# The second layer's modulation columns move from up projections to down projections

## The chip, the core and the metric

One core of a Trainium2 chip runs the whole program. The metric is device time in microseconds, from 1894.69 to 1894.86 in three runs of the kernel before, 1894.77 in the median.

Engines are called TensorE (PE in the profile, PEld its weight loads), VectorE (DVE), ScalarE (ACT), GpSimd (POOL) and SyncE (SP).

## What is computed

Two blocks of a sequence model in float32, on 512 tokens of width 1024: the first with stick-breaking and gated linear attention and a convolutional feed-forward network, the second with two layers (pooling and grid attention in one, an mLSTM in the other), each with its own feed-forward network. The layers of the second block are modulated by a condition `c`:

```python
    cond = jax.nn.silu(c)
    for layer in range(DEPTH_2):
        mod = cond @ ada_w[layer] + ada_b[layer]
        sh1, sc1, g1, sh2, sc2, g2 = jnp.split(mod, 6, axis=-1)
        h = modulate(rms_norm_2(x), sh1, sc1)
        ...
        x = x + g1[:, None, :] * y
        h = modulate(rms_norm_2(x), sh2, sc2)
        x = x + g2[:, None, :] * swiglu(h, ffn_w1[layer], ffn_w3[layer], ffn_w2[layer])
```

`ada_w` is 2 x 1024 x 6144 numbers, 50 MB. The product has one row, and the kernel does not give it to TensorE.

## The kernel before, in words

**Stages and chunks.** The program is a list of stages, each of some chunks of weights. The three feed-forward networks (FFN) are called by a prefix: none for the first block's, `e_` and `o_` for the two layers of the second. Each has two halves of an up and a down stage: `up0`, `down0`, `up1`, `down1`, and so on. An up stage has 11 chunks of 48 matmuls of 512 columns, a down stage 8 chunks of 33. Activations lie as 128 x 512 tiles, 8 of them for a width of 1024.

**One chunk.** SyncE loads weights into one of two `raw` slots. ScalarE rounds them into `wh` (`hi_part`, L514), always 2048 columns. GpSimd takes the difference `raw - wh` into `wl` (L2386), 1408 columns in a down stage and 2048 in an up stage; for `pool_u`, the stage behind `down1`, and a few others it does so in four instructions of 512 (L2396). TensorE multiplies three times (`wh` and `wl` by the high part of the input, `wh` by the low part). It starts a chunk when `lo_done` says that GpSimd is through, and when the chunk two before has been drained from PSUM. `hi_part` of the next chunk waits for the end of the chunk before the present one, whose slot it takes.

**Draining a down chunk.** VectorE adds the result to the residual tile `h` (L691, L692). Where a norm follows the stage (`down1`, `e_down1`), `hi_only` has ScalarE square and scale the tile of the chunk before (`tile_act`, L231 to L240), and VectorE adds the square to a running sum and forms the low part (`tile_dve`, L258, L263, L266). `down1` needs two sums, of x and of the scaled x, so three operations on each engine; `e_down1` needs two. At the start of the next stage TensorE takes the sum over partitions (`norm_sum_pe`, L379).

**Modulation.** The 96 columns of `mod` (48 for each layer, 128 numbers each) are sums on VectorE: `ada_dve` (L856) multiplies a 128 x 1024 tile of `ada_w`, loaded into one of four slots, by the condition and accumulates along the row. They are spread over stages by the table `ADA_OF`: one a chunk in `out` and `att_out` (4 each), two a chunk in `up0`, `up1`, `e_up0` and `e_up1` (22 each). `ada_load` (L849) issues the 512 KB load for a column from ScalarE's queue in the up stages, from SyncE's in `out` and `att_out`; it waits until the sum that last used the slot is done. Each engine takes its instructions in the order in which the program lists them, so a load that waits holds what stands behind it on ScalarE. `mod_dve` adds the bias for a layer, of layer 0 ahead of `down1`, of layer 1 ahead of `e_down1`.

Of the kernel before, what the change touches and what calls it, by code (L numbers as in the profile page):

```python
# [92 lines left out]
def build(nc, xT, w2048, w1024, w1408, ada, c_d, par_d, cst_d, gla_d, rope_d, pool_d, outT):  # L93
    with ExitStack() as ctx:
# [99 lines left out]
        GQ_SQ = [arena[:, 8, :], arena[:, 9, :]]  # L194
        GQ_ACC = arena[:, 15, :]
        RSTD = arena[:, 30, :]
# [451 lines left out]
        def hi_only(a, stage):  # L648
# [4 lines left out]
            def body(c, slot, l):  # L653
                if not (KIND[stage] == "D" and is_static(l) and l == 0):
                    hi_part(a, c + 1, 1 - slot)
                if norm and KIND[stage] == "D":
                    if is_static(l) and l == 0:
                        return
                    a.wait_ge(drained, c)
                    tile_act(a, norm, l - 1, 1 - slot)  # L660
                elif norm:
                    a.wait_ge(res_half, l + (HALF_OF[stage] + 1))
                    tile_act(a, norm, l * 2, 0)
                    a.wait_ge(drained, c + 1)
                    tile_act(a, norm, l * 2 + 1, 1)
            if norm:
                chunk_loop(a, stage, body, hi=3)
                chunk_loop(a, stage, body, lo=3, hi=COUNT[stage] - last)
# [16 lines left out]
        def drain_residual(v, stage, gate=None):  # L685
# [29 lines left out]
            if norm:  # L715
# [5 lines left out]
                chunk_loop(v, stage, body, lo=1, hi=2)  # L721
                chunk_loop(v, stage, body, lo=2)
                tile_dve(v, norm, KT - 1, (C0[stage] + KT - 1) % 2 if KIND[stage] == "D" else 1)
# [23 lines left out]
        def ada_first(a, stage):  # L747
            for l in range(2):
                ada_load(a, stage, (C0[stage] + l) % 2, l)

        def up_act(a, stage):
# [6 lines left out]
            def body(c, slot, l, ahead=True, open_=True):  # L758
# [17 lines left out]
                a.activation(zh[:, bass.ds(l, 1), :], HID[:, slot:slot + 1, :], ACT.Copy).then_inc(hid_hi, 1)  # L776
                if stage in ADA_OF and not (is_static(l) and l + 2 >= HALF):
                    ada_load(a, stage, slot, l + 2)
# [10 lines left out]
        def up_dve(v, stage):  # L789
# [4 lines left out]
            def body(c, slot, l):  # L794
# [17 lines left out]
                else:  # L812
# [4 lines left out]
                                zh[:, bass.ds(l, 1), :].bitcast(F), ALU.subtract).then_inc(drained, 1)  # L817
                if stage in ADA_OF:
                    ada_dve(v, stage, slot, l)
            if stage in NORM_INTO and not first:  # L820
                chunk_loop(v, stage, body, hi=1)
                chunk_loop(v, stage, body, lo=1)
            else:
# [8 lines left out]

        ADA_OF = {"out": (0, 1), "up0": (4, 2), "up1": (4 + 2 * HALF, 2), "att_out": (ADA_M, 1),
                  "e_up0": (ADA_M + 4, 2), "e_up1": (ADA_M + 4 + 2 * HALF, 2)}

        def ada_at(stage, slot, l, i):

            first, each = ADA_OF[stage]
            A = l * each + (first + i)
            if is_static(A):  # L840
                return A, A % ADA_SLOTS
            return A, (first + i + each * ((slot + C0[stage]) % 2)) % ADA_SLOTS

        def ada_load(sp, stage, slot, l):
            for i in range(ADA_OF[stage][1]):
                A, at = ada_at(stage, slot, l, i)
                if not (is_static(A) and A < ADA_SLOTS):
                    sp.wait_ge(ada_done, A - (ADA_SLOTS - 1))
                sp.dma_start(ada_raw[:, at, :], ada[bass.ds(A, 1), :, :].rearrange("a p n -> p (a n)")  # L849
                             ).then_inc(ada_full[at], 16)  # L850

        def ada_dve(v, stage, slot, l):
            for i in range(ADA_OF[stage][1]):
                A, at = ada_at(stage, slot, l, i)
                v.wait_ge(ada_full[at], A * 4 + (16 - 4 * at))
                v.scalar_tensor_tensor(ada_raw[:, at, :], ada_raw[:, at, :], 1.0, cond_row[:, :], ALU.mult, ALU.mult,  # L856
# [1561 lines left out]
        def _(a):  # L2418
# [13 lines left out]
            a.wait_ge(drained, end_of("up1"))  # L2432
            a.dma_start(ROPE[:, :, :], rope_d.rearrange("p (a t) -> p a t", t=T)).then_inc(rope_in, 16)
# [31 lines left out]
        def _(v):  # L2465
# [29 lines left out]
            for i in range(2):  # L2495
# [194 lines left out]
```

## Time and profile before

| | |
|---|---|
| median of three runs | 1894.77 us |
| profiled execution, span from first to last instruction | 1893.4 us (its full time isn't shown apart) |
| TensorE busy | 1874.5 us, 99% |
| VectorE, ScalarE, GpSimd busy | 905.8, 751.5, 775.2 us |
| granted TensorE clock | 1.000 |
| modulation sums (L856) | 96, 188.7 us |
| their loads | 96 of 512 KB, 5.3 us to landing in the median |
| weight subtraction on GpSimd (L2386) | 158, 648.8 us |
| `down1`, first to last matmul | 687.55 to 747.4 us |
| `e_up0`, `e_down0`, `e_up1`, `e_down1` | 919.4 to 1281.3 us |

A time in the trace is in microseconds from the start of the span. Matmuls are pipelined: each record is some 389 ns long, but the next one starts 227 ns after it, so a busy share near 100% doesn't show how fast TensorE runs; the chain of waits, which merges matmuls that follow one another, does. A record of VectorE or GpSimd begins where the instruction was issued to the engine, so time in which it was held up inside is part of its length.

### The profile page before, as it was taken

The page shows a single profiled execution, that of the slowest core. Times are in us where ns is not written, and L with a number is a line of the kernel's source. Part 1 is how long each engine was busy: PE and PEld are TensorE (multiplying, and loading weights), DVE is VectorE, ACT ScalarE, POOL GpSimd, SP SyncE. Part 2 cuts the span into 40 slices and gives each one's busy share as a digit, 9 for nine tenths or more (in the row PEclk, how much of TensorE's full clock was granted, in tenths as well). Part 3 has the DMA queues.
Part 4 walks back from the last instruction along what each step waited for, and adds up shares of the span by engine and source line. Part 5 has one row for each costly group of instructions (what it writes and reads, how often), then busy time and mean ns, then how long its engine had stood idle before and what let it go on. Part 6 is the DMA issues. An engine that isn't in the chain of part 4 may idle for free.

```text
span 1893.4 us, 24348 instructions
## 1 busy us (share of the span) xinstructions
PE 1874.5 (99%) x9258; PEld 1524.5 (81%) x9258; DVE 905.8 (48%) x1235; ACT 751.5 (40%) x948; POOL 775.2 (41%) x254
## 2 busy tenths in 40 slices
PE   9999999999999999999999999999999999999999
PEld 6877788878888887656788888888998888888887
DVE  6455525676504653875666236628665551111110
ACT  6455344443323335465532322244377342222221
POOL 3322323434344435312443444343486433444333
PEclk9999999999999999999999999999999999999999
DMA  5222212445436434202455255433322223132322
GB/s 218 73 73 68 67 56 81 175 164 194 147 105 222 177 124 148 89 23 71 154 197 179 97 187 192 149 106 100 112 62 75 89 94 106 68 111 100 110 74 92
DMA packets 46508, 224.02 MB, mean 118 GB/s; under 512 B 4944, under 2 KB 9296, under 8 KB 31840
## 3 DMA queue, kind: packets, MB, share of 16 engines
q1 hardware_dynamic: 32896, 173.94, 27.1%
q10 hardware_dynamic: 13536, 49.03, 6.7%
q8 instruction: 53, 0.87, 0.2%
q14 instruction: 23, 0.19, 0.0%
HBM read 220.81 MB, written 2.13 MB: 118 GB/s over the span
## 4 chain that ended last, share of the span: by engine, by line
PE 86%; DVE 4%; issue 3%; POOL 3%; ACT 2%; DMA 1%; SPq 0%; ACTq 0%; POOLq 0%; DVEq 0%
PE pairs L552 41%; PE pairs L593 18%; PE pairs L1151 4%; PE pairs L628 3%; PE pairs L530 2%; PE pairs L919 2%; PE pairs L584 2%; PE pairs L931 2%; POOL arena L2133 2%; PE pairs L422 1%; POOL wl L2386 1%; DMA raw<-in_w 1%; PE pairs L617 1%; PE aux L1751 1%; PE pairs L442 1%
## 5 line engine op out<-in xcount | busy, mean ns | idle before, releaser
L2386 POOL TENSOR_TENSOR wl<-raw,wh 128x2048 fp32r<-128x2048 f32 (+2 forms) x158 | 648.8, 4106 | 929.0 <-ACT wh L514 929.0
L514 ACT ACTIVATE wh<-raw 128x2048 fp32r<-128x2048 f32 x171 | 326.7, 1911 | 300.9 <-PE pairs L593 208.1
L552 PE MATMUL pairs<-xh,wh 128*128 128x512 f32 x1120 | 436.1, 389 | 1.8 <-DVE aux L813 1.5
L552 PE MATMUL pairs<-xl,wh 128*128 128x512 f32 x1120 | 435.7, 389 | 0.0
L552 PE MATMUL pairs<-xh,wl 128*128 128x512 f32 x1120 | 435.7, 389 | 0.0
L552 PEld LDWEIGHTS pairs<-xh,wh 128*128 128x128 f32 x1120 | 210.2, 188 | 46.1 <-DVE aux L813 1.9
L552 PEld LDWEIGHTS pairs<-xh,wl 128*128 128x128 f32 x1120 | 210.2, 188 | 43.7
L552 PEld LDWEIGHTS pairs<-xl,wh 128*128 128x128 f32 x1120 | 210.2, 188 | 43.5
L593 PE MATMUL pairs<-zl,wh 128*128 128x512 f32 x518 | 201.6, 389 | 0.0
L593 PE MATMUL pairs<-zh,wl 128*128 128x512 f32 x518 | 201.5, 389 | 0.0
L593 PE MATMUL pairs<-zh,wh 128*128 128x512 f32 x518 | 201.5, 389 | 0.0
L856 DVE SCALAR_TENSOR_TENSOR arena<-arena,cond_row 128x1024 f32<-128x1024 f32 x96 | 188.7, 1997 | 0.0
L771 ACT ACTIVATE arena<-pairs 128x512 f32<-128x512 f32 x42 | 25.2, 600 | 323.7 <-PE pairs L552 304.5
L813 DVE TENSOR_TENSOR aux<-arena,pairs 128x512 f32<-128x512 f32 x64 | 44.6, 696 | 227.4 <-ACT arena L771 212.8
L692 DVE SCALAR_TENSOR_TENSOR h<-pairs,mod,h 128x512 f32 (+1 forms) x48 | 35.9, 750 | 222.7 <-PE pairs L593 179.4
L593 PEld LDWEIGHTS pairs<-zh,wh 128*128 128x128 f32 x518 | 97.2, 188 | 20.5
L593 PEld LDWEIGHTS pairs<-zh,wl 128*128 128x128 f32 x518 | 97.2, 188 | 20.2
L593 PEld LDWEIGHTS pairs<-zl,wh 128*128 128x128 f32 x518 | 97.2, 188 | 20.1
L2396 POOL TENSOR_TENSOR wl<-raw,wh 128x512 fp32r<-128x512 f32 x36 | 49.8, 1414 | 119.5 <-ACT wh L514 119.5
L816 DVE TENSOR_TENSOR zl<-aux,zh 128x512 f32 (+1 forms) x66 | 45.7, 692 | 92.4 <-ACT zh L776 92.4
L691 DVE TENSOR_TENSOR h<-pairs,h 128x512 f32 (+1 forms) x24 | 16.5, 692 | 96.9 <-PE pairs L593 81.1
L231 ACT ACTIVATE arena<-h 128x512 f32<-128x512 f32 (+1 forms) x40 | 25.0, 626 | 86.9 <-DVE h L692 55.9
(370 smaller groups left out, 2992.3 us busy)
## 6 DMA issues: line engine op xcount, KB each, us to landing
raw<-in_w SPq DMA_DIRECT2D x113, 1024.0 KB, 5.0
arena<-in_ada ACTq DMA_DIRECT2D x88, 512.0 KB, 5.3
raw<-in_w SPq DMA_DIRECT2D x48, 704.0 KB, 4.1
raw<-in_w SPq DMA_DIRECT2D x12, 512.0 KB, 3.6
arena<-in_ada SPq DMA_DIRECT2D x8, 512.0 KB, 5.3
arena<-mx_rows SPq DMA_DIRECT2D x16, 256.0 KB, 3.6
h<-in_xT SPq DMA_DIRECT2D x4, 512.0 KB, 9.0
outT<-h SPq DMA_DIRECT2D x8, 256.0 KB, 5.4
```

The source lines that it names most:

```text
L514: a.activation(wh[:, slot, :], raw[:, slot, :], ACT.Copy).then_inc(hi_done, 1)
L530: mm = p.matmul(pairs[:, 2 * slot + m, :], w[:, slot, at:at + P], (xh, xl)[part][:, k, :], start=(k == 0 and w is wh and part == 0), stop= ...
L552: mm = p.matmul(pairs[:, 2 * slot + m, :], w[:, slot, at:at + P], src[part][:, k, :], start=(k == 0 and w is wh and part == 0), stop=(k == ...
L584: mm = p.matmul(dst, src[part][:, k, tb * P:(tb + 1) * P], w[:, slot, at:at + n], start=(k == 0 and w is wh and part == 0), stop=(k == KT ...
L593: mm = p.matmul(pairs[:, 2 * slot + m, :], w[:, slot, k * P:(k + 1) * P], src[part][:, k, :], start=(k == ks[0] and w is wh and part == 0) ...
L628: mm = p.matmul(pairs[:, 2 * slot + m, :], w[:, slot, k * P:(k + 1) * P], src[part][:, k, :], start=(k == ks[0] and w is wh and part == 0) ...
L813: v.tensor_tensor(HID[:, slot, :], ACTV[:, slot, :], pairs[:, 2 * slot + 1, :], ALU.mult).then_inc(hid_done, 1)
L816: v.tensor_tensor(zl[:, bass.ds(l, 1), :], HID[:, slot:slot + 1, :], zh[:, bass.ds(l, 1), :].bitcast(F), ALU.subtract).then_inc(drained, 1)
L856: v.scalar_tensor_tensor(ada_raw[:, at, :], ada_raw[:, at, :], 1.0, cond_row[:, :], ALU.mult, ALU.mult, accum_out=mod_raw[:, bass.ds(A, 1) ...
L1151: mm = p.matmul(pairs[:, 2 * slot + m, :], w[:, slot, at:at + P], x[:, k, :], start=(k == 0 and w is wh and x is xh), stop=(k == KT - 1 an ...
L2386: g.tensor_tensor(wl[:, slot, 0:w], raw[:, slot, 0:w], wh[:, slot, 0:w].bitcast(F), ALU.subtract).then_inc(lo_done, 1)
L2396: ins = g.tensor_tensor(wl[:, slot, at:at + QW], raw[:, slot, at:at + QW], wh[:, slot, at:at + QW].bitcast(F), ALU.subtract)
```

## The change

The table becomes a plan with a running number, since columns are no longer summed in their order in `ada_w`. In the order of the program: `out` 4, `up0` 22, `down0` 16 (two for each of its 8 chunks), `up1` 22, `down1` 14 (chunks 0 to 6), `att_out` 4, `e_up0` 4 (chunks 0 and 1), `e_down1` 10 (chunks 0 to 4). `e_up1` has none. In the down stages `hi_only` issues the loads for chunk l+1 behind `hi_part` and ahead of `tile_act`, and `drain_residual` sums behind the residual addition and ahead of `tile_dve`. Layer 1's bias is added in two parts, the second (`mod_rest_dve`) behind the norm that follows `e_down1`. The accumulator `GQ_ACC` moves, since the slots for `ada_w` are now in use during `down1`.

```diff
-        GQ_ACC = arena[:, 15, :]
+        GQ_ACC = arena[:, 23, :]
...
             def body(c, slot, l):
                 if not (KIND[stage] == "D" and is_static(l) and l == 0):
                     hi_part(a, c + 1, 1 - slot)
+                if KIND[stage] == "D" and stage in ADA_OF and not (is_static(l) and l + 1 >= ADA_OF[stage][2]):
+                    ada_load(a, stage, 1 - slot, l + 1)
                 if norm and KIND[stage] == "D":
...
+            if KIND[stage] == "D" and stage in ADA_OF:
+                if stage == "e_down1":
+                    a.wait_ge(mm_done, C0[stage])
+                ada_first(a, stage)
+                if not norm:
+                    ada_load(a, stage, (C0[stage] + 1) % 2, 1)
...
                     add(l, pairs[:, 2 * slot:2 * slot + 1, :]).then_inc(drained, 1)
-                    if stage in ADA_OF:
+                    if stage in ADA_OF and not (is_static(l) and l >= ADA_OF[stage][2]):
                         ada_dve(v, stage, slot, l)
...
-        ADA_OF = {"out": (0, 1), "up0": (4, 2), "up1": (4 + 2 * HALF, 2), "att_out": (ADA_M, 1),
-                  "e_up0": (ADA_M + 4, 2), "e_up1": (ADA_M + 4 + 2 * HALF, 2)}
+
+        ADA_PLAN = [("out", 0, 1, 4), ("up0", 4, 2, HALF), ("down0", ADA_M, 2, KT), ("up1", 4 + 2 * HALF, 2, HALF),
+                    ("down1", ADA_M + 16, 2, 7), ("att_out", ADA_M + 30, 1, 4), ("e_up0", ADA_M + 34, 2, 2),
+                    ("e_down1", ADA_M + 38, 2, 5)]
...
+            n = 32 if layer else 48
+            v.wait_ge(ada_done, ADA_SCALES if layer else ADA_OF["down1"][3])
+            v.tensor_tensor(mod[:, layer, 0:n], mod[:, layer, 0:n], pc("ada_b", 48 * layer, n), ALU.add
+                            ).then_inc(mod_done, 1)
...
+        def mod_rest_dve(v):
+
+            v.wait_ge(ada_done, ADA_Q)
+            v.wait_ge(mod_done, 4)
+            v.tensor_tensor(mod[:, 1, 32:48], mod[:, 1, 32:48], pc("ada_b", 80, 16), ALU.add).then_inc(mod_done, 1)
+            v.wait_ge(mod_done, 5)
+            v.tensor_scalar(mod[:, 1, 32:40], mod[:, 1, 32:40], 1.0, None, ALU.add).then_inc(mod_done, 1)
+            v.wait_ge(mod_done, 6)
...
             norm_dve(v, "n_o1")
+            mod_rest_dve(v)
             conv5_dve(v)
```

ScalarE at the start of `down1`, before: the last operation of `up1`, the weights of `down1`'s chunk 2, tile 0, the weights of chunk 3.

```order
L776 ACTIVATE zh<-aux 128x512 [waits consts,hid_done]
L514 ACTIVATE wh<-raw 128x2048 [waits mm_done,raw_full1]
L231 ACTIVATE arena<-h 128x512 [waits sq_sum,drained]
L237 ACTIVATE arena<-h,par 128x512 [waits gsc_done]
L240 ACTIVATE xh<-h,gsc 128x512
L514 ACTIVATE wh<-raw 128x2048 [waits mm_done,raw_full0]
```

The same with the change (L790 is the old L776).

```order
L790 ACTIVATE zh<-aux 128x512 [waits consts,hid_done]
L874 DMA arena<-in_ada 128x1024 [waits ada_done] x4
L514 ACTIVATE wh<-raw 128x2048 [waits mm_done,raw_full1]
L874 DMA arena<-in_ada 128x1024 [waits ada_done] x2
L231 ACTIVATE arena<-h 128x512 [waits sq_sum,drained]
L237 ACTIVATE arena<-h,par 128x512 [waits gsc_done]
L240 ACTIVATE xh<-h,gsc 128x512
L514 ACTIVATE wh<-raw 128x2048 [waits mm_done,raw_full0]
```

Six loads, each with a wait for a sum (`ada_done`), now stand ahead of the weights of chunk 3, four of them ahead of those of chunk 2.

VectorE in `down1`, before: the additions for chunks 0 and 1 and tile 0's three operations.

```order
L691 TENSOR_TENSOR h<-pairs,h 128x512 [waits mm_done,zeroed]
L691 TENSOR_TENSOR h<-pairs,h 128x512 [waits mm_done]
L258 TENSOR_TENSOR arena<-arena 128x512 [waits sq_done]
L263 TENSOR_TENSOR arena<-arena 128x512 [waits gq_done]
L266 SCALAR_TENSOR_TENSOR xl<-h,gsc,xh 128x512 [waits u_hi]
```

The same with the change (L702 is the old L691, L881 the old L856).

```order
L702 TENSOR_TENSOR h<-pairs,h 128x512 [waits mm_done,zeroed]
L881 SCALAR_TENSOR_TENSOR arena,mod<-arena,cond_row 128x1024 [waits ada_full0]
L881 SCALAR_TENSOR_TENSOR arena,mod<-arena,cond_row 128x1024 [waits ada_full1]
L702 TENSOR_TENSOR h<-pairs,h 128x512 [waits mm_done]
L881 SCALAR_TENSOR_TENSOR arena,mod<-arena,cond_row 128x1024 [waits ada_full2]
L881 SCALAR_TENSOR_TENSOR arena,mod<-arena,cond_row 128x1024 [waits ada_full3]
L258 TENSOR_TENSOR arena<-arena 128x512 [waits sq_done]
L263 TENSOR_TENSOR arena<-arena 128x512 [waits gq_done]
L266 SCALAR_TENSOR_TENSOR xl<-h,gsc,xh 128x512 [waits u_hi]
```

Two sums stand behind each addition, ahead of the tile operations; each waits for its load (`ada_full`).

## Rows read from the trace of the kernel before

**Rows 1.** Waits of TensorE: line waited for, us in total, times, longest.

```profile
PE aux L1513 <- DVE arena L1518: 2.3, 1, 2.3
...
PE aux L390 <- POOL wl L2396: 0.2, 1, 0.2
```

**Rows 2.** Chain that ended last, at the FFNs: start us, us, what.

```profile
508.03 7.48 PE pairs L628 x33
...
695.03 44.89 PE pairs L593 x198
...
1101.79 119.68 PE pairs L552 x528
...
1710.44 119.68 PE pairs L552 x528
```

**Rows 3.** Timeline of VectorE, end of up1 and down1: start us, us.

```profile
695.54 0.08 DVE L856 DVE_READ_ACCUMULATOR arena<-arena,cond_row 128x1 f32 x1
...
697.63 0.69 DVE L691 TENSOR_TENSOR h<-pairs,h 128x512 f32<-128x512 f32 x1
...
704.36 0.75 DVE L266 SCALAR_TENSOR_TENSOR xl<-h,gsc,xh 128x512 fp32r<-128x512 f32 x1
```

**Rows 4.** All sums (ns min/median/max), then GpSimd and VectorE in e_up0.

```profile
L856 DVE SCALAR_TENSOR_TENSOR arena<-arena,cond_row x96: 1212/1216/4522, 353.1 to 1228.2; 128x1024 f32<-128x1024 f32 x96
...
949.30 4.61 POOL L2386 TENSOR_TENSOR wl<-raw,wh 128x2048 fp32r<-128x2048 f32 x1 [8.44 <-ACT wh L514]
...
950.49 4.50 DVE L856 SCALAR_TENSOR_TENSOR arena<-arena,cond_row 128x1024 f32<-128x1024 f32 x1
```

**Rows 5.** Timeline of GpSimd, down1.

```profile
697.12 3.22 POOL L2386 TENSOR_TENSOR wl<-raw,wh 128x1408 fp32r<-128x1408 f32 x1 [3.82 <-ACT wh L514]
704.61 3.59 POOL L2386 TENSOR_TENSOR wl<-raw,wh 128x1408 fp32r<-128x1408 f32 x1 [4.26 <-ACT wh L514]
```

**Rows 6.** Timeline of VectorE, last sum of up0.

```profile
516.02 0.08 DVE L856 DVE_READ_ACCUMULATOR arena<-arena,cond_row 128x1 f32 x1
```

**Rows 7.** Timelines of VectorE and ScalarE, a load's wait in up0.

```profile
412.84 0.08 DVE L856 DVE_READ_ACCUMULATOR arena<-arena,cond_row  x1
...
413.49 0.60 ACT L764 ACTIVATE arena<-pairs 128x512 f32<-128x512 f32 x1 [3.70 <-DVE arena L856]
```

**Rows 8.** Timeline of ScalarE, down1 chunk 3's weights and tile 1.

```profile
702.61 1.92 ACT L514 ACTIVATE wh<-raw 128x2048 fp32r<-128x2048 f32 x1 [2.39 <-PE pairs L593]
704.44 0.61 ACT L231 ACTIVATE arena<-h 128x512 f32<-128x512 f32 x1
...
706.18 0.20 ACT L243 ACTIVATE shs<-mod 128x8 f32<-128x8 f32 x1
```

**Rows 9.** GpSimd's quarters alone, then with VectorE's tile operations between them.

```profile
752.02 5.01 POOL L2396 TENSOR_TENSOR wl<-raw,wh 128x512 fp32r<-128x512 f32 x4 [4.50 <-ACT wh L514]
...
891.29 5.94 POOL L2396 TENSOR_TENSOR wl<-raw,wh 128x512 fp32r<-128x512 f32 x4 [5.40 <-ACT wh L514]
...
892.87 1.52 DVE L258 TENSOR_TENSOR arena<-arena 128x512 f32<-128x512 f32 x1
894.31 1.77 DVE L266 SCALAR_TENSOR_TENSOR xl<-h,mod,xh 128x512 fp32r<-128x512 f32 x1
```

**Rows 10.** Chain that ended last, start of pool_u.

```profile
747.57 1.07 PE aux L390 x16
...
752.95 0.87 PE aux L379 x2
...
753.84 0.70 ACT arena L332
```

**Rows 11.** Timeline of VectorE, behind the convolution of the mLSTM layer.

```profile
1341.20 0.74 DVE L2016 TENSOR_SCALAR arena<-pairs,par 40x512 f32<-40x512 f32 x1 [2.21 <-PE pairs L2009]
```

**Rows 12.** All loads for the sums.

```profile
DMA to landing us min/median/max: 3.5/5.3/8.5
```

**Rows 13.** Busy times, pool_u to att_q1: PE, PEld, DVE, ACT, POOL, PEclk, DMA, GB/s.

```profile
747.50:886.70 139.20, 132.50 (x665) 87.52 (x666) 102.58 (x153) 77.39 (x129) 32.42 (x25) 1.00 0.20 71
```

More of the change, by code:

```diff
@@ L665, in body @@
                     tile_act(a, norm, l * 2 + 1, 1)
+            if KIND[stage] == "D" and stage in ADA_OF:
[4 more added lines that the diff above has]
+                    ada_load(a, stage, (C0[stage] + 1) % 2, 1)
             if norm:
                 chunk_loop(a, stage, body, hi=3)
-                chunk_loop(a, stage, body, lo=3, hi=COUNT[stage] - last)
+                last_ada = ADA_OF[stage][2] - 1 if stage in ADA_OF and KIND[stage] == "D" else COUNT[stage] - last
+                chunk_loop(a, stage, body, lo=3, hi=last_ada)
+                for l in range(last_ada, COUNT[stage] - last):
+                    body(C0[stage] + l, (C0[stage] + l) % 2, l)
                 if KIND[stage] == "D":
@@ L721, in drain_residual @@
                 chunk_loop(v, stage, body, lo=1, hi=2)
-                chunk_loop(v, stage, body, lo=2)
+                last_ada = ADA_OF[stage][2] if stage in ADA_OF and KIND[stage] == "D" else COUNT[stage]
+                chunk_loop(v, stage, body, lo=2, hi=last_ada)
+                for l in range(last_ada, COUNT[stage]):
+                    body(C0[stage] + l, (C0[stage] + l) % 2, l)
                 tile_dve(v, norm, KT - 1, (C0[stage] + KT - 1) % 2 if KIND[stage] == "D" else 1)
@@ L747, in ada_first @@
         def ada_first(a, stage):
-            for l in range(2):
+            for l in range(1 if KIND[stage] == "D" else 2):
                 ada_load(a, stage, (C0[stage] + l) % 2, l)
@@ L776, in body @@
                 a.activation(zh[:, bass.ds(l, 1), :], HID[:, slot:slot + 1, :], ACT.Copy).then_inc(hid_hi, 1)
-                if stage in ADA_OF and not (is_static(l) and l + 2 >= HALF):
+                if stage in ADA_OF and ADA_OF[stage][2] == HALF and not (is_static(l) and l + 2 >= HALF):
                     ada_load(a, stage, slot, l + 2)
@@ L817, in body @@
                                 zh[:, bass.ds(l, 1), :].bitcast(F), ALU.subtract).then_inc(drained, 1)
-                if stage in ADA_OF:
+                if stage in ADA_OF and (ADA_OF[stage][2] == HALF or is_static(l) and l < ADA_OF[stage][2]):
                     ada_dve(v, stage, slot, l)
@@ L821, in up_dve @@
                 chunk_loop(v, stage, body, hi=1)
-                chunk_loop(v, stage, body, lo=1)
+                if stage in ADA_OF:
+                    chunk_loop(v, stage, body, lo=1, hi=2)
+                    chunk_loop(v, stage, body, lo=2)
+                else:
+                    chunk_loop(v, stage, body, lo=1)
             else:
@@ L831, in build @@
         mod_raw = mod[:, :, :].rearrange("p a b -> p (a b)")
-        ADA_OF = {"out": (0, 1), "up0": (4, 2), "up1": (4 + 2 * HALF, 2), "att_out": (ADA_M, 1),
-                  "e_up0": (ADA_M + 4, 2), "e_up1": (ADA_M + 4 + 2 * HALF, 2)}
-        def ada_at(stage, slot, l, i):
[L838 to L842, printed above, removed]
+        ADA_PLAN = [("out", 0, 1, 4), ("up0", 4, 2, HALF), ("down0", ADA_M, 2, KT), ("up1", 4 + 2 * HALF, 2, HALF),
+                    ("down1", ADA_M + 16, 2, 7), ("att_out", ADA_M + 30, 1, 4), ("e_up0", ADA_M + 34, 2, 2),
+                    ("e_down1", ADA_M + 38, 2, 5)]
+        ADA_OF, ADA_Q = {}, 0
+        for ada_stage, ada_col, ada_each, ada_n in ADA_PLAN:
+            ADA_OF[ada_stage] = (ada_col, ada_each, ada_n, ADA_Q)
+            ADA_Q += ada_each * ada_n
+        ADA_SCALES = ADA_OF["e_down1"][3]
+        def ada_at(stage, slot, l, i):
+            first, each, _, q0 = ADA_OF[stage]
+            q = l * each + (q0 + i)
+            if is_static(q):
+                return q, q + (first - q0), q % ADA_SLOTS
+            return q, q + (first - q0), (q0 + i + each * ((slot + C0[stage]) % 2)) % ADA_SLOTS
         def ada_load(sp, stage, slot, l):
             for i in range(ADA_OF[stage][1]):
-                A, at = ada_at(stage, slot, l, i)
-                if not (is_static(A) and A < ADA_SLOTS):
-                    sp.wait_ge(ada_done, A - (ADA_SLOTS - 1))
+                q, A, at = ada_at(stage, slot, l, i)
+                if not (is_static(q) and q < ADA_SLOTS):
+                    sp.wait_ge(ada_done, q - (ADA_SLOTS - 1))
                 sp.dma_start(ada_raw[:, at, :], ada[bass.ds(A, 1), :, :].rearrange("a p n -> p (a n)")
@@ L853, in ada_dve @@
             for i in range(ADA_OF[stage][1]):
-                A, at = ada_at(stage, slot, l, i)
-                v.wait_ge(ada_full[at], A * 4 + (16 - 4 * at))
+                q, A, at = ada_at(stage, slot, l, i)
+                v.wait_ge(ada_full[at], q * 4 + (16 - 4 * at))
                 v.scalar_tensor_tensor(ada_raw[:, at, :], ada_raw[:, at, :], 1.0, cond_row[:, :], ALU.mult, ALU.mult,
@@ L2431, in _ @@
                 hi_only(a, f"down{i}")
-            a.wait_ge(drained, end_of("up1"))
+            a.wait_ge(ada_done, ADA_OF["att_out"][3])
             a.dma_start(ROPE[:, :, :], rope_d.rearrange("p (a t) -> p a t", t=T)).then_inc(rope_in, 16)
```

4 lines of the change are left out of this document (1 added, 3 removed).

## The prediction

> **What bounds the kernel now.** I read the waits of TensorE first, since its busy time is nearly the whole span. The longest single one is 2.3 us, and the only one at the stages that the change touches is 0.2 us behind GpSimd at the start of pool_u [rows 1]. So TensorE sets the time, and a change of work on the other engines counts only where it makes TensorE wait or stops a wait.
>
> The chain of waits says whether TensorE runs slower where the sums lie. e_up1 holds 22 of them and o_up1 holds none; both run 528 matmuls in 119.68 us, 226.7 ns each, without a break [rows 2].
>
> Then I looked at what a sum costs VectorE. Alone it takes 1.22 us; beside its last 0.08, the accumulator's read [rows 3], the next instruction starts, so a second sum follows after 1.14. But the longest took 4.52 [rows 4]. The two lines below it there give the reason: a sum that starts at 950.49, while GpSimd's subtraction runs from 949.30 to 953.91, ends at 954.99, 1.08 after it. A sum and GpSimd's subtraction exclude each other, and so do the tile operations, which also read two inputs from SBUF. The other direction shows in down1: GpSimd asks at 704.61 while the tile operation of 704.36 to 705.11 runs, and needs 3.59 us instead of 3.22, so it ends 3.09 after the holder [rows 3, 5]. The residual addition, with one input in PSUM, runs at 697.63 in 0.69 inside GpSimd's 697.12 to 700.34: it is not excluded.
>
> **The change part by part.** Forty of 96 sums move: 18 leave e_up0 and 22 leave e_up1; 16 go to down0, 14 to down1, 10 to e_down1. Their count, and that of the loads, stays.
>
> *Removed from the second FFN's up stages.* VectorE saves up to 4.52 + 1.22 us per chunk of 10.88, but TensorE waits for none of it: the stage without sums has the same 119.68 [rows 2]. Gain: 0. The Trainium skill (TensorE: Matmul & The Clock Gate, section "Wait — 56ns, not 53.3ns?") gives 215.7 ns for back-to-back matmuls of 512 columns, against 226.7 here; if the sums made that gap, two stages of 528 would gain 11.6 us (an estimate). The row of o_up1 decides: the gap is there without them.
>
> *down0.* ScalarE now waits ahead of chunk 2 for up0's last sum, read out at 516.10 [rows 6], to issue the loads. After such a wait it starts its next operation 0.57 later (412.92 to 413.49) [rows 7], so the weight conversion starts at 516.67, GpSimd asks 2.0 later (702.61 to 704.61 [rows 5, 8]) at 518.67, and ends 521.9. TensorE wants chunk 2 at 508.03 + 2 x 7.48 = 522.99 [rows 2]. Cover 1.1 us; cost 0. In the later chunks an addition and two sums, 0.7 + 2 x 1.14, hold GpSimd until 3.0 after the chunk's end, so it ends 3.1 later, at 6.1 of 7.48: cost 0. Only the last wait is for a larger subtraction, 4.61 [rows 4] for up1's first weights: 3.0 + 4.5 = 7.5 against 7.48. Cost 0.1.
>
> *down1, chunk 3.* Here each chunk already has three tile operations. Chunk 0 ends 695.03, and 44.89 / 6 = 7.48 per chunk [rows 2]: chunk 1 ends 702.51, chunk 2 709.99.
> - up1's last sum ends 695.62 [rows 3]. ScalarE, which must issue chunk 1's loads behind it, converts chunk 2's weights from 696.19; GpSimd asks at 698.19.
> - VectorE adds at 697.63 as before and wants its first sum at 698.24. Its load needs only sums of up1's chunk 9, and could land as late as 701.4 without harm. GpSimd was first: it ends 701.41, the sums 702.49 and 703.63. (Were the sum first, the second would still end near 703.6.)
> - ScalarE must issue chunk 2's loads behind these: free at 704.20. Then tile 0's three operations, 1.74 us (704.44 to 706.18) [rows 8]. Chunk 3's weights are converted from 705.94, not 702.6.
> - GpSimd asks at 707.94. VectorE has added chunk 1 (703.6), summed twice (704.2, 705.3) and is in tile 0's third operation until 708.39. GpSimd ends 708.39 + 3.09 = 711.48; TensorE starts 711.54 in place of 709.99. **Cost 1.5.** If GpSimd asks 0.3 earlier it goes ahead of that operation: 0.9. If each ScalarE wait is 0.2 longer: 1.9.
>
> *down1, the hand-over to pool_u.* GpSimd's 3.22, two sums at 1.14, three tile operations (1.9) and the addition's 0.61 make 8.0 us per chunk in one line, against 7.48. VectorE falls back some 0.5 a chunk from chunk 3 on, and adds chunk 6 about 1.3 late. With the cost above, chunk 6 ends 741.46 and chunk 7 748.94. pool_u's subtraction, in four quarters, is asked for at 743.5, where VectorE is at chunk 6's sums. Alone the quarters take 5.01; two operations let in between made 5.94 of them, 0.46 each [rows 9]. So: held 0.9 by the first sum, 5.01, the second sum let in 1.0, two tile operations 0.9: 751.3. TensorE, ready at 748.94, waits **2.4**. Without VectorE's lag it would be 750.7. pool_u starts 3.7 later than at 747.57 [rows 10]. All of it counts: TensorE's norm sum at 752.95 is followed by ScalarE at once, so the chain of pool_u starts there. VectorE's last tile operations also end some 4 us later, but the norm sum moves with pool_u and still comes after them.
>
> *e_down1.* Two tile operations: 3.22 + 2.28 + 1.3 + 0.6 = 7.4, only five chunks, its first loads need no earlier sum. GpSimd ends near 6.1 of 7.48: cost 0.
>
> *The late bias.* Two instructions of at most 16 columns ahead of the convolution. Even as long as a 512-column operation (0.75 [rows 3]) they make 1.5, and VectorE idles 2.21 at 1341 [rows 11]. Cost 0; without that cover up to 1.5.
>
> *Loads.* They move with the sums, 1 MB a chunk beside the weights; the sums are used a chunk after the issue, some 11 us, against 3.5 to 8.5 to landing [rows 12]. Cost 0. The new place of the second accumulator moves nothing.
>
> Sum: 3.7 + 0.1 = 3.8. The profiled execution's span is 1893.4; its full time isn't shown apart, and the runs' median is 1894.8, so 1.4 lies around the span and is kept. **Forecast 1898.6 us**, +0.20%. By the bounds (chunk 3 from 0.9 to 1.9; pool_u from 1.4, with no lag and one tile operation less let in, to 2.6, with 0.2 more lag; less the 0.2 that was there, and up1's 0.1) its own range is 1897.0 to 1899.2.
>
> **The rivals.** 0.2% is 3.8 us, about what a measurement of this kernel can tell from no change.
> 1. ScalarE is not held by its load issues, which use none of its arithmetic. Then weights are converted on time, and with less lag only VectorE's hold on the quarters is left, 2.0: 1896.8. Against: ScalarE stood idle for 3.70 us ahead of the operation at 413.49, behind a sum [rows 7]. 0.10.
> 2. Not slower: what follows pool_u takes up the delay. Its place is 747.5 to 886.7, where TensorE has 6.7 us idle [rows 13] and waits for VectorE and ScalarE, 2.3 at L1513 [rows 1]; a later TensorE would only wait less. It decides if VectorE's tile sums, not TensorE's arrival, release the norm sum. Then only down0's 0.1 is left: 1894.9. Against: the chain passes through that norm sum [rows 10]. 0.10.
> 3. The lag reaches TensorE within down1. Where the conversion or the residual addition slips behind in chunks 4 to 7 too, each gives 8.0 - 7.48 = 0.5: 2.1 more, 1900.7. My steps leave only some 0.3 us of cover at chunk 7. 0.12.
> 4. A drop of TensorE's clock after the new waits. The granted clock is 1.00 (2.4 GHz) through the stretch with the 2.3 us wait [rows 1, 13], and mine are no more than 2.4. At the lower level (1.2 GHz) pool_u's first 48 matmuls would take another 10.9: 1909.5. The Trainium skill (TensorE: Matmul & The Clock Gate, Part 1) says an idle array falls to that level; the trace shows none. 0.03.
> 5. Faster: the up stages gain after all and down1 hides its sums. 3.6 ns off each of their 1056 matmuls would be 3.8 us: 1891.0. Against: the stage without sums shows no such gain [rows 2]. 0.05.
>
> **How the numbers follow.** The forecast has 0.60. It lies on the 0.2% line: 0.28 of it below, 0.32 above, since costs I put at nothing can only add. Same: 0.28 + 0.10 + 0.10 = 0.48. Slower: 0.32 + 0.12 + 0.03 = 0.47. Faster 0.05. The range 1895.5 to 1901.5 takes in the forecast with its bounds, rivals 1 and 3, and leaves out 0.18.
>
> **What would show it.** In the profile after: TensorE's wait behind GpSimd's subtraction at chunk 3 of down1, 0.9 to 1.9 us; the weight conversion there some 3 us after the end of chunk 1; in later chunks sums of 2 to 4 us, each ending 1.1 after GpSimd; the four quarters for pool_u at 7 to 8 us, and a wait at L390 near 2; e_up0 and e_up1 unchanged at 226.7 ns. I am wrong if down1 shows no wait of TensorE, if VectorE's tile operations there keep 0.7 us, if up0's stretch or pool_u's chain changes length, or if the up stages of the second FFN get shorter.

## The result and the profile after

The changed kernel takes **1900.36 us** (median of 7, 1900.15 to 1901.57) against 1894.93 (7, 1894.69 to 1895.29): ratio 1.003, 95% interval 1.0019 to 1.0041. It is 5.4 us slower, where 3.8 were forecast; the time lies inside the stated range, and 1.2 above the upper end (1899.2) of the forecast's own bounds. The profiled execution has a span of 1899.4 us, 6.0 more than that of before, while VectorE's busy time fell from 905.8 to 878.8 us and that of the sums from 188.7 to 138.3.

First the waits of TensorE after the change (line waited for: us in total, times, longest), those that are new or answer to [rows 1]:

```profile
PE aux L1548 <- DVE arena L1553: 2.3, 1, 2.3
PE aux L390 <- POOL wl L2431: 2.2, 1, 2.2
...
PE pairs L593 <- POOL wl L2421: 1.5, 1, 1.5
...
PE pairs L563 <- DVE arena L1972: 0.6, 1, 0.6
PE pairs L552 <- POOL wl L2421: 0.5, 2, 0.3
```

The forecast had 2.4 at L390 and 1.5 in down1. The 0.6 at L563, in the mLSTM layer, it did not have. Of the two waits at L552 the one of 0.3 stands in the profile of before too; the other, of 0.2, is at up1's first matmul. The chain that ended last (start us, us, what), from down1's chunk 3 to the norm sum of pool_u, then the second FFN's second up stage:

```profile
708.02 3.62 POOL wl L2421
711.76 30.22 PE pairs L593 x132
...
744.06 7.54 POOL wl L2431 x4
751.64 1.07 PE aux L390 x16
752.72 0.43 PE pairs L442
753.15 0.43 PE pairs L443
...
756.14 0.42 PE pairs L444
756.56 0.23 PE pairs L442
...
758.62 0.87 PE aux L379 x2
759.52 0.70 ACT arena L332
...
1107.27 119.68 PE pairs L552 x528
```

Two things are to be seen. The up stage that lost 22 sums (e_up1, at 1107.27) lasts 119.68 us as it did with them [rows 2]: nothing came from there. And the matmuls between L390 and the norm sum take 0.43 us each for a while, not 0.23; from L390 to L379 it is 6.98 us where it was 5.38 [rows 10]. The busy times by stretch, with the granted clock as the third number from the end, say why:

```profile
751.60:753.00 1.40, 1.35 (x18) 0.73 (x19) 1.40 (x3) 0.23 (x1) 0.00 (x0) 1.00 0.00 0
753.00:754.50 1.50, 1.50 (x5) 1.22 (x4) 1.50 (x3) 1.50 (x3) 0.00 (x0) 0.51 0.51 104
754.50:756.00 1.50, 1.50 (x5) 1.13 (x5) 1.50 (x4) 1.50 (x2) 0.00 (x0) 0.50 0.88 317
756.00:758.70 2.70, 2.70 (x12) 2.19 (x11) 0.47 (x1) 1.72 (x2) 2.19 (x2) 0.92 1.00 413
```

1.4 us after the wait of 2.2 the clock falls to 0.50 (1.2 GHz), and comes back at about 756.4. Eight matmuls at 0.43 instead of 0.23 are 1.6 us, the whole difference.

The timelines of GpSimd, ScalarE and VectorE in down1 (start us, us):

```profile
708.02 3.60 POOL L2421 TENSOR_TENSOR wl<-raw,wh 128x1408 fp32r<-128x1408 f32 x1 [6.45 <-ACT wh L514]
...
744.06 7.53 POOL L2431 TENSOR_TENSOR wl<-raw,wh 128x512 fp32r<-128x512 f32 x4 [2.75 <-ACT wh L514]
```

```profile
704.27 0.63 ACT L231 ACTIVATE arena<-h 128x512 f32<-128x512 f32 x1 [6.01 <-DVE arena L881]
...
706.04 1.91 ACT L514 ACTIVATE wh<-raw 128x2048 fp32r<-128x2048 f32 x1
```

```profile
707.82 0.74 DVE L266 SCALAR_TENSOR_TENSOR xl<-h,gsc,xh 128x512 fp32r<-128x512 f32 x1
...
712.64 4.23 DVE L881 SCALAR_TENSOR_TENSOR arena<-arena,cond_row 128x1024 f32<-128x1024 f32 x1
...
738.15 3.71 DVE L258 TENSOR_TENSOR arena<-arena 128x512 f32<-128x512 f32 x1
...
744.78 2.31 DVE L881 SCALAR_TENSOR_TENSOR arena<-arena,cond_row 128x1024 f32<-128x1024 f32 x1
```

ScalarE stood 6.01 us behind the sums and converted chunk 3's weights at 706.04 instead of 702.61 [rows 8]; GpSimd then met VectorE's third tile operation. Sums and tile operations of 2.3 to 4.2 us are those that met a subtraction. The rule of the Trainium skill (SBUF — State Buffer, section "Who interferes with whom") says the same: a VectorE instruction with two inputs in SBUF and a GpSimd instruction that reads SBUF exclude each other whole. The sum of 712.64 agrees: it ends 1.1 us after GpSimd's 712.32 to 715.79.

Last, the late bias on VectorE, and TensorE's first matmul at L563:

```profile
1307.28 0.32 DVE L900 TENSOR_TENSOR mod<-mod,par 128x16 f32<-128x16 f32 x1
1307.63 0.17 DVE L902 TENSOR_SCALAR mod<-mod 128x8 f32<-128x8 f32 x1
```

```profile
1337.29 0.36 PE L563 MATMUL pairs<-wh,xh 128*128 128x256 f32 x1 [0.63 <-DVE arena L1972]
```

### The profile page after: what moved, and what is told of

The parts are those of the page before. It is cut to its first block, busy times and chain, and to the rows that moved or that the text cites. A ratio compares the mean times of both kernels' runs of the same rounds, so it can differ in the third digit from the quotient of the medians.

```text
span 1899.4 us, 24163 instructions
## 1 busy us (share of the span) xinstructions
PE 1876.2 (99%) x9258; PEld 1525.1 (80%) x9258; DVE 878.8 (46%) x1237; ACT 752.2 (40%) x948; POOL 787.0 (41%) x254
## 4 chain that ended last, share of the span: by engine, by line
PE 69%; issue 16%; POOL 6%; DVE 6%; ACT 2%; DMA 1%; POOLq 0%; SPq 0%; ACTq 0%; DVEq 0%
PE pairs L552 29%; PE pairs L593 15%; POOL wl L2421 4%; PE pairs L1186 4%; PE pairs L954 2%; PE pairs L584 2%; PE pairs L628 2%; PE pairs L966 2%; PE pairs L530 2%; POOL arena L2168 2%; PE pairs L422 1%; DMA raw<-in_w 1%; PE pairs L617 1%; PE aux L1786 1%; DVE aux L1989 1%
## 5 line engine op out<-in xcount | busy, mean ns | idle before, releaser
L2421 POOL TENSOR_TENSOR wl<-raw,wh 128x2048 fp32r<-128x2048 f32 (+2 forms) x158 | 658.6, 4168 | 923.1 <-ACT wh L514 923.1
L552 PE MATMUL pairs<-xh,wh 128*128 128x512 f32 x1120 | 436.2, 389 | 1.9 <-DVE aux L827 1.5
L552 PE MATMUL pairs<-xh,wl 128*128 128x512 f32 x1120 | 435.7, 389 | 0.0
L552 PE MATMUL pairs<-xl,wh 128*128 128x512 f32 x1120 | 435.7, 389 | 0.0
L552 PEld LDWEIGHTS pairs<-xh,wh 128*128 128x128 f32 x1120 | 210.2, 188 | 46.7 <-DVE aux L827 1.9
L552 PEld LDWEIGHTS pairs<-xl,wh 128*128 128x128 f32 x1120 | 210.2, 188 | 43.7
L552 PEld LDWEIGHTS pairs<-xh,wl 128*128 128x128 f32 x1120 | 210.2, 188 | 43.6
L593 PE MATMUL pairs<-zh,wh 128*128 128x512 f32 x518 | 201.6, 389 | 1.5 <-POOL wl L2421 1.5
L593 PE MATMUL pairs<-zl,wh 128*128 128x512 f32 x518 | 201.6, 389 | 0.0
L593 PE MATMUL pairs<-zh,wl 128*128 128x512 f32 x518 | 201.6, 389 | 0.0
L881 DVE SCALAR_TENSOR_TENSOR arena<-arena,cond_row 128x1024 f32<-128x1024 f32 x96 | 138.3, 1473 | 0.0
L703 DVE SCALAR_TENSOR_TENSOR h<-pairs,mod,h 128x512 f32<-128x512 f32 (+1 forms) x48 | 35.9, 750 | 205.6 <-PE pairs L593 157.2
L593 PEld LDWEIGHTS pairs<-zh,wh 128*128 128x128 f32 x518 | 97.2, 188 | 22.4 <-DVE h L702 1.9
L593 PEld LDWEIGHTS pairs<-zh,wl 128*128 128x128 f32 x518 | 97.2, 188 | 20.1
L593 PEld LDWEIGHTS pairs<-zl,wh 128*128 128x128 f32 x518 | 97.2, 188 | 20.1
L231 ACT ACTIVATE arena<-h 128x512 f32<-128x512 f32 x40 | 25.2, 629 | 109.5 <-DVE h L703 55.2
L258 DVE TENSOR_TENSOR arena<-arena 128x512 f32<-128x512 f32 x40 | 65.2, 1630 | 0.0
```

Source lines behind the costliest of these rows:

```text
L258: v.tensor_tensor(SQ_ACC, SQ_ACC, SQ[slot], ALU.add).then_inc(sq_acc, 1)
L552: mm = p.matmul(pairs[:, 2 * slot + m, :], w[:, slot, at:at + P], src[part][:, k, :], start=(k == 0 and w is wh and part == 0), stop=(k == ...
L593: mm = p.matmul(pairs[:, 2 * slot + m, :], w[:, slot, k * P:(k + 1) * P], src[part][:, k, :], start=(k == ks[0] and w is wh and part == 0) ...
L2421: g.tensor_tensor(wl[:, slot, 0:w], raw[:, slot, 0:w], wh[:, slot, 0:w].bitcast(F), ALU.subtract).then_inc(lo_done, 1)
```

## The experiments

Theory: down1's 14 sums make chunk 3's wait (by ScalarE's queue), the late hand-over (by VectorE's lag), and the clock's drop behind it; the late bias makes the 0.6 at L563; the rest of the move costs next to nothing and gains nothing. Rivals: the sums of down0 or the new places of the loads; the exclusion of VectorE and GpSimd alone, whatever ScalarE does; a drop of the clock that has nothing to do with TensorE's idle time.

**Down1's sums back.** In the table of the plan, with e_up0's loops ended at their ninth chunk:

```diff
-("down1", ADA_M + 16, 2, 7), ("att_out", ADA_M + 30, 1, 4), ("e_up0", ADA_M + 34, 2, 2),
+("att_out", ADA_M + 16, 1, 4), ("e_up0", ADA_M + 20, 2, 9),
```

> The 14 sums of down1 go back to e_up0 (now 9 chunks with sums); down0, e_down1 and the late bias stay as in the changed kernel. Theory (down1's sums make the three delays between 695 and 759 us: 1.5 at chunk 3, 2.2 at the hand-over to pool_u, 1.6 of TensorE's clock behind that): TensorE has no wait above 0.3 us in down1 or at L390, the granted clock stays 1.00 up to the norm sum, and the time is that of the kernel before plus 0.2 (up1's first weights) and 0.6 (late bias): 1895.7, between 1895.3 and 1896.2. Rival (the delay belongs to down0's sums or to the new places of loads in general): 1899 or more. Rival (the second FFN's up stages had gained and hid something): e_up0 gets longer than 119.68 less its old parts, and the time stays near 1900.

1896.23 (1895.63 to 1896.49), before 1895.10; ratio 1.0007 (0.9997 to 1.0016). TensorE's only wait from 690 to 760 us is the old one:

```profile
PE aux L390 <- POOL wl L2436: 0.2, 1, 0.2
```

pool_u starts at 747.52, and at L563 the 0.6 is whole. So down1's sums make the waits in down1 and at L390 and the drop, and the ten sums of e_down1 and the moved loads cost nothing that TensorE shows. The median is 0.5 over the theory's value, just above its bounds.

The sums of down0 are not free, and they account for 0.3 of it, since the theory had 0.2 at up1. TensorE's first matmuls of down0, up1 and down1, before and in this run:

```profile
507.87 0.39 PE L628 MATMUL pairs<-zh,wh 128*128 128x512 f32 x1
567.71 0.39 PE L552 MATMUL pairs<-xh,wh 128*128 128x512 f32 x1
687.39 0.39 PE L628 MATMUL pairs<-zh,wh 128*128 128x512 f32 x1
```

```profile
507.33 0.39 PE L628 MATMUL pairs<-zh,wh 128*128 128x512 f32 x1
567.49 0.50 PE L552 MATMUL pairs<-xh,wh 128*128 128x512 f32 x1 [0.16 <-POOL wl L2426]
687.34 0.39 PE L628 MATMUL pairs<-zh,wh 128*128 128x512 f32 x1
```

The places at 687 are alike only because this execution came to down0 0.54 earlier. From down0 to down1 it takes 180.01 us, before 179.52. All nine kernels with sums in down0 take 179.97 to 180.01 in their profiles, and the three without them 179.52 each (the kernel before, and below with one and with two extra subtractions). The 0.45 to 0.49 between them lie at up1's start. GpSimd's subtraction of up1's first weights, before and with the change:

```profile
562.49 4.59 POOL L2386 TENSOR_TENSOR wl<-raw,wh 128x2048 fp32r<-128x2048 f32 x1 [4.27 <-ACT wh L514]
562.27 5.49 POOL L2421 TENSOR_TENSOR wl<-raw,wh 128x2048 fp32r<-128x2048 f32 x1 [3.37 <-ACT wh L514]
```

With the change it is held behind the chunk's second sum and ends at 567.76; up1's first matmul comes at 567.82, 0.55 after the one ahead of it instead of 0.23, and the second another 0.1 late. No run took the sums out of down0 alone; the cause is read from these rows.

**Fewer chunks with sums in down1.** Five instead of seven, with e_up0's loops ended at their fourth chunk:

```diff
-("down1", ADA_M + 16, 2, 7), ("att_out", ADA_M + 30, 1, 4), ("e_up0", ADA_M + 34, 2, 2),
+("down1", ADA_M + 16, 2, 5), ("att_out", ADA_M + 26, 1, 4), ("e_up0", ADA_M + 30, 2, 4),
```

> Down1 keeps sums in chunks 0 to 4 only (10); the other 4 go to e_up0. Theory (VectorE, 0.5 us a chunk behind, meets the quarters for pool_u with sums left over): chunk 3's wait of 1.5 stays, VectorE has caught up by chunk 7, the wait at L390 is 0.3 or less and without a drop of the clock behind it: 2.0 less, and 1.6 less again where the clock had dropped: 1896.8 to 1898.4. Rival (the wait at L390 is carried over from chunk 3's delay): it stays above 1.5, near 1900.

1897.65 (1897.29 to 1898.05), inside the theory's bounds. The wait at chunk 3 stays, that at L390 is gone:

```profile
PE pairs L593 <- POOL wl L2426: 1.5, 1, 1.5
```

The quarters take 5.39 us, since VectorE has no sums left beside them, and pool_u starts at 749.16, 1.6 later than before. The delay at chunk 3 is kept to the end but makes no second one. The wait at L390 belongs to the sums of the last two chunks.

**Loads that need not wait.** The loop that issues them ends a step later to match:

```diff
-                if KIND[stage] == "D" and stage in ADA_OF and not (is_static(l) and l + 1 >= ADA_OF[stage][2]):
-                    ada_load(a, stage, 1 - slot, l + 1)
+                ahead = 0 if stage == "down1" else 1
+                if KIND[stage] == "D" and stage in ADA_OF and not (is_static(l) and (
+                        l + ahead >= ADA_OF[stage][2] or l + ahead == 0)):
+                    ada_load(a, stage, 1 - slot if ahead else slot, l + ahead)
```

> In down1 ScalarE issues chunk l's two loads in its own step l instead of a step ahead, so that it never waits there for sums that are not done; the sums themselves stay. Theory (ScalarE, held by its load issues, converts chunk 3's weights too late): the 1.5 us wait at chunk 3 vanishes or is below 0.3, the weight conversions start within 0.6 of each chunk's end; VectorE is still behind at the end, so a wait of 1.5 to 2.0 at L390 stays: 1898.3 to 1898.9 with the clock's drop after it, 1897.1 without. Rival (VectorE and GpSimd excluding each other is enough to make that wait, ScalarE does not matter): the wait of 1.5 at chunk 3 stays, 1900.4. Rival (loads issued this late land after VectorE asks for them): VectorE waits for a DMA in down1 and TensorE's wait at L390 grows over 2.5.

1899.28 (1898.72 to 1900.02). ScalarE converts each chunk's weights at the end of the chunk before it, and TensorE has no wait within down1:

```profile
702.59 1.92 ACT L514 ACTIVATE wh<-raw 128x2048 fp32r<-128x2048 f32 x1 [2.39 <-PE pairs L593]
```

```profile
749.47 1.07 PE L390 MATMUL aux<-raw,shs 128*32 128x256 f32 x16 [2.10 <-POOL wl L2433]
```

So the 1.5 is ScalarE's queue: with the same sums under the same subtractions it is gone. The hand-over's wait stays, as the theory had it. But the time is 0.4 above its upper value, which has the clock's drop in it; in the profiled execution, the fastest of the ten at 1898.72, the clock stayed at 1.00, and for that case the theory had 1897.1. The stretch from down0 to down1 has its 0.5 here too, and the profile shows two losses behind the hand-over. ScalarE, late by the last tile, starts the norm at L332 2.40 later than before the change, though pool_u starts only 1.90 later. And the norm has an addition of two SBUF tiles on VectorE (L483), which met GpSimd's next quarters (755.01 to 760.03) and took 1.5, against 0.9 before the change:

```profile
759.11 1.48 DVE arena L483
```

This is the theory's exclusion at a place that it had not looked at; the next experiment shows it too.

**TensorE kept busy through the wait.** PSUM bank 3 of aux is read by nothing there, and the products are dropped:

```diff
+            if name == "n_final":
+                for i in range(9):
+                    p.matmul(aux[:, 3, :], zh[:, 0, 0:P], zh[:, 1, :], start=True, stop=True)
             p.wait_ge(lo_done, c + 1)
```

> The changed kernel, with nine more matmuls of 512 columns (9 x 226.7 ns = 2.0 us) from down1's finished hidden tiles into a PSUM bank that nothing reads, between down1's last matmul and pool_u's first. TensorE then stands idle some 0.2 us there instead of 2.2. Theory (the drop of the granted clock to half behind L390 follows the idle time): the clock stays 1.00 from 750 to 760 us, the norm sum comes 5.4 us after the first matmul of L390 instead of 7.0, and the executions scatter less: 1898.8 if every execution of the changed kernel had the whole drop, 1899.6 if most had a part of it. Rival (the drop comes from what runs there, the sixteen 128x32 matmuls, or from the later time): half clock as before, 1900.4.

```profile
749.13 2.20 PE L436 MATMUL aux<-zh 128*128 128x512 f32 x9
751.52 1.07 PE L390 MATMUL aux<-raw,shs 128*32 128x256 f32 x16 [0.19 <-POOL wl L2434]
...
752.86 0.40 PE L446 MATMUL pairs<-xh,wl 128*128 128x512 f32 x1
...
756.73 1.02 PE L379 MATMUL aux<-arena,cst 128*128 128x512 f32 x2
```

From L390 to the norm sum it is 5.21 us, as before the change by the same view (747.57 to 752.78), with every matmul at full clock. One profile alone would not show it, since the same wait also comes without a drop (see the late bias). But of the eight executions none lies over 0.3 above the median, and of the nine with these matmuls and the bias moved, further below, none over 0.5, where two of the change's seven lie 0.9 and 1.2 above theirs. The drop follows the idle time. Yet the median is 1900.20 (1899.91 to 1900.49), 0.16 below the change's and 0.6 over the theory's upper value. The same profile says where 0.4 of that is:

```profile
756.40 5.02 POOL L2434 TENSOR_TENSOR wl<-raw,wh 128x512 fp32r<-128x512 f32 x4 [4.93 <-ACT wh L517]
```

```profile
760.66 1.31 DVE L486 TENSOR_TENSOR arena<-arena 128x512 f32<-128x512 f32 x1 [0.79 <-ACT arena L338]
```

L486 is the line L483 of the changed kernel. GpSimd's quarters start when ScalarE has converted the weights, whatever TensorE does; where the norm sum comes early, the addition falls under them (1.31 here, 0.87 before the change), and where the clock drops, it comes behind them:

```profile
762.39 0.69 DVE L483 TENSOR_TENSOR arena<-arena 128x512 f32<-128x512 f32 x1 [0.79 <-ACT arena L338]
```

So of the drop's 1.6 some 0.6 are given back at once, and an execution with it is about 1.0 longer: the profiled one took 1901.25, and five of the seven took 1900.15 to 1900.60, as with TensorE kept busy. That those five had no drop is inferred from their times. This is why taking the drop away hardly moves the median.

**The idle time alone, without any sum in down1.** In the kernel before, one or two extra subtractions ahead of pool_u's quarters (here two):

```diff
+                    for i in (23, 25) if stage == "pool_u" and l == 0 else ():
+                        g.tensor_tensor(arena[:, i, :], raw[:, slot, 0:QW], wh[:, slot, 0:QW].bitcast(F),
+                                        ALU.subtract)
```

> The kernel before, with one more subtraction of a quarter (1.25 us, its result unused) on GpSimd ahead of pool_u's four quarters. TensorE waits 1.4 at L390 instead of 0.2, with no sum in down1. Theory (a TensorE that has stood idle for some us can have its clock halved for a while behind it): 1896.3 without a drop, 1897.9 with one of 1.6; the wait itself passes on whole, since the norm sum follows TensorE. Rival (what follows pool_u takes a delay up): 1895.1 to 1895.5.

> The kernel before, with two more subtractions of a quarter (2.5 us, results unused) on GpSimd ahead of pool_u's four. TensorE waits 2.7 at L390. Theory: 1897.6 without a drop of the clock, 1899.2 with one of 1.6, executions of both kinds possible; the drop shows as 0.50 granted from about 1.3 us after the wait on, in matmuls of 0.43 us instead of 0.23. Rival (the drop needs the sums of down1, not the idle time): 1897.6 in every execution, 1.00 throughout.

With one: 1895.86 (1895.45 to 1896.47), 0.95 more than before. TensorE waits 1.4, and the clock stays at 1.00. With two: 1899.24 (1897.46 to 1900.24), 4.3 more. Busy times by stretch with two:

```profile
748.00:750.00 2.00, 0.00 (x0) 0.83 0.53 131
750.00:752.00 2.00, 2.00 (x17) 0.50 1.06 410
752.00:754.00 2.00, 2.00 (x5) 0.50 0.95 367
754.00:756.00 2.00, 2.00 (x6) 0.50 0.84 223
756.00:758.00 2.00, 2.00 (x10) 0.96 0.74 299
```

```profile
PE aux L390 <- POOL wl L2399: 3.1, 1, 3.1
```

The wait of 3.1 ends under a clock that has fallen already, and it stays down for some 7 us. The wait is 2.9 longer than before; alone it would give 1897.8. Three of the eleven executions lie about there, at 1897.46 to 1897.89, the others 0.9 to 2.4 above 1897.8. No sum of down1 is needed for the drop. A wait of 1.4 showed none here; of those of 2.1 and 2.2 us the change and the early bias (below) showed one in their profiles, the loads and the late bias none; the 3.1 showed one. The delay passes on but for 0.2: with one extra subtraction TensorE's wait is 1.2 longer than before, which makes pool_u start 0.87 later, since this execution came to down1 0.36 earlier, and the norm's L467 starts 0.70 later. The Trainium skill (TensorE: Matmul & The Clock Gate, Part 1) says that an array left idle falls to the lower level; the rows of the 3.1 agree, at 0.50.

**The late bias.** Ahead of the norm n_o1, or behind the convolution:

```diff
-            norm_dve(v, "n_o1")
             mod_rest_dve(v)
+            norm_dve(v, "n_o1")
             conv5_dve(v)
```

> The changed kernel with the late bias (two instructions of 16 and 8 columns, 0.58 us of VectorE) ahead of the norm n_o1 in place of behind it. There VectorE idles about 4.3 us for the norm's rows. Theory (the convolution's start is on VectorE's path, and TensorE's new wait of 0.6 us at L563 is that): the wait at L563 is gone and the time falls by 0.55: 1899.8. Rival (the wait at L563 comes from a later norm sum or from the later accumulator): it stays, 1900.4.

```diff
-            mod_rest_dve(v)
             conv5_dve(v)
+            mod_rest_dve(v)
```

> The changed kernel with the late bias behind the convolution instead of ahead of it; VectorE idles about 2.2 us there for TensorE's gates. Theory (the 0.58 us ahead of the convolution is the wait at L563): that wait is gone, 0.55 less, 1899.8. Rival (VectorE had a stall of 0.49 with no releaser inside the convolution when the bias was moved ahead of the norm, and would have one here too, because code stands elsewhere): the wait at L563 stays near 0.5, 1900.4.

Both medians say nothing, 1901.05 (1899.91 to 1901.54) and 1900.49 (1899.22 to 1901.22): the clock's drops scatter them by over 1.5 us. The two profiled executions show both kinds: after the same wait of 2.2 at L390 the early bias (1901.35) has the drop, with 6.98 us from L390 to the norm sum, and the late bias (1899.22) has none, with 5.38:

```profile
751.14 1.07 PE aux L390 x16
...
756.52 0.87 PE aux L379 x2
```

The profiles say more. Behind the convolution the wait at L563 is gone. Ahead of the norm the convolution starts 0.49 earlier (20.85 us after L390's first matmul instead of 21.34), but VectorE then stops in it, with its own last instruction as the only releaser, and TensorE still waits 0.5:

```profile
1326.83 1.23 DVE L1972 TENSOR_SCALAR arena<-pairs 128x1024 f32<-128x1024 f32 x1 [0.49 <-DVE arena L1989]
```

What held it there was not found. To weigh the bias without the clock's scatter, the nine matmuls and the place behind the convolution together (both diffs above):

> The nine extra matmuls ahead of pool_u and the late bias behind the convolution, both in the changed kernel: without the clock's drops, which scattered the executions of the run with the bias alone, the bias can be weighed. Theory (0.58 us of VectorE ahead of the convolution are 0.55 of the time): the wait at L563 is gone and the time is 0.55 below the run with the nine matmuls alone, 1899.65, scatter below 0.7. Rival (TensorE's wait moves on behind the convolution): 1900.2, with a wait of 0.5 somewhere between 1340 and 1350 us.

1899.78 (1899.62 to 1900.20), 0.42 below the nine matmuls alone; against the kernel before as it ran beside each, 4.66 in place of 5.29. The bias is 0.4 to 0.6, and nothing behind the convolution takes it back.

**Three remedies together**, the plan with five chunks, the loads without a wait and the bias behind the convolution (diffs above):

> Three remedies in one, with 36 of the 40 sums still moved: sums in down1's chunks 0 to 4 only (4 go to e_up0), each chunk's loads there issued in its own step, the late bias behind the convolution. Theory (chunk 3's wait, the hand-over to pool_u with VectorE's lag behind it, and the late bias are the whole cost, and the removal from the second FFN's up stages gains nothing): no wait over 0.3 us in down1, at L390 or at L563, and the time of the kernel before, 1894.9 to 1895.3. Rival (the moved sums cost something more, by the loads or by the port): 1896 or more. Rival (the emptier up stages gain after all): 1893 or less.

1895.24 (1894.98 to 1895.59), before 1895.12; ratio 1.0001 (0.9992 to 1.0010). The view of TensorE's waits lists none between 690 and 760 us nor between 1290 and 1345, and pool_u starts at 747.51. The theory's value, and neither rival's: with 36 of the 40 sums moved, the time is that of the kernel before, within the interval. Down0's sums still cost their 0.46 in this profile (179.98 us from down0 to down1), of which 0.12 come back at the start of pool_u; 0.3 are too little for the medians to show. What the up stages no longer do is worth nothing to a TensorE that did not wait for it.

## Why the prediction was right in kind and too small

Delays against the kernel before, in the profiled executions (first matmul of down0, down1 and pool_u, ScalarE's first operation on the norm sum at L332, VectorE's L467 at the end of that norm, which is L470 with TensorE kept busy, and the span):

```
                        down0    down1   pool_u    L332    L467    span
change                  -0.21    +0.25    +4.07   +5.68   +5.50    +6.0
TensorE kept busy       -0.36    +0.10    +3.95   +3.95   +4.38    +4.9
loads without a wait    -0.47    -0.02    +1.90   +2.40   +3.00    +3.5
five chunks             -0.56    -0.10    +1.59   +1.59   +1.59    +2.1
three remedies          -0.40    +0.06    -0.06   -0.02   -0.07    -0.1
```

The first column is scatter: the profiled execution of the kernel before came late to down0, where nothing has changed yet. What a stage costs is the difference of two columns.

- **Up stages: 0.** Right: 119.68 with and without sums, and the three remedies gain nothing.
- **e_down1, loads: 0.** Right, by the run without down1's sums.
- **down0: 0.1, at up1's first weights. Right in place and kind, too small:** 0.46. GpSimd's end and TensorE's need were set against each other at 7.5 and 7.48 us, a tie, and here the tie cost TensorE more than the 0.1 that was put: its first matmul came 0.32 late and its second another 0.1.
- **Chunk 3: 1.5.** Right in size and in kind. The weights' conversion was put at 705.94 (706.04), GpSimd at 707.94 to 711.48 (708.02 to 711.62), TensorE at 711.54 (711.76), all of it in a down1 that starts 0.25 later. The loads without a wait show that ScalarE's queue makes it, so rival 1 falls.
- **Hand-over: 2.4, pool_u 3.7 later.** Right: 2.2, and 3.8 from the start of down1 on, quarters 7.53. Five chunks take the wait away. Rival 3 falls: L593 has one wait, at chunk 3.
- **"The norm sum moves with pool_u": right, and rival 2 falls, but the step stopped there.** Behind the norm sum the addition at L483 shares GpSimd's quarters, and took 0.44 longer where the clock held (1.31 against 0.87). The exclusion that the prediction used in down1 was not carried on to the next pair of instructions on the delayed path. The text's own sign of being wrong, "if up0's stretch or pool_u's chain changes length", came here: from L390 to L332 it is 7.88 us with the change's drop and 6.27 before.
- **The late bias: failed.** It was put at 0 because VectorE idles 2.21 us [rows 11]. That idle time lies behind the convolution, and the bias stands ahead of it; the convolution is VectorE's own path, and TensorE waits for its end at L563. The text's own other case, "without that cover up to 1.5", held, at 0.55: in the change's profile TensorE is 5.48 late at that layer's L390 and 6.05 at L563.
- **Rival 4, the clock (0.03): its reason failed.** "The granted clock is 1.00 (2.4 GHz) through the stretch with the 2.3 us wait [rows 1, 13], and mine are no more than 2.4" took one wait of that length as proof for another. A drop came, in part of the executions; it lasted 3.4 us and not 48 matmuls, and cost 1.6 less 0.6, far from the 10.9 that rival 4 had.

The sum with these sizes, without the drop: 0.46 + 3.85 + 0.44 + 0.55 = 5.3 us, for down0, down1 with its hand-over, the addition at L483 and the bias. The run with TensorE kept busy lies 5.29 above the kernel before as it ran beside it. The forecast's 3.8 lacks 0.36 at down0, 0.15 at pool_u, 0.44 at L483 and 0.55 for the bias.

That the time lies inside the stated range is in part luck: above 1899.2 the range was there for rival 3, whose waits within down1 did not come, and terms that were put at nothing or at 0.1 filled the place.

## What to carry to other kernels

Idle time covers an instruction only if it lies ahead of the same consumer: follow the engine's order from the new instruction to the next engine that waits, and look for the gap on that path. Work taken from a stage where the bound engine never waits gains nothing, and where it goes it competes with the queue that feeds that engine; an in-order queue that issues loads behind a wait holds everything behind it. A wait of some 2 us on TensorE is to be priced with and without a drop of its clock, since the same wait of 2.2 showed both. And compare lengths of stages, not places on the time axis: executions differed by up to 0.7 us ahead of the first changed stage, which hid a cost of 0.5 in it.

## What the runs showed of the hardware beyond that

The clock's drop does not start with the wait: after 2.2 us of idle time it came 1.4 us behind the wait's end and lasted 3.4 us (matmuls of 512 columns at 0.43 us), after 3.1 us it came within the wait and lasted some 7. A kernel whose TensorE has such a wait scatters more: 2.8 us over eleven executions with the wait of 3.1, 0.6 over eight with TensorE kept busy.
